# Seven quarter products for eight in ten of the eleven gate groups of the FFN behind the first attention

## The reference, cut to what matters

```
def swiglu(h, w_in, w_out):
    g, u = jnp.split(h @ w_in, 2, axis=-1)
    return (jax.nn.silu(g) * u) @ w_out

h = adaln(x, norm_g[i, 2], mod[:, 2, 0], mod[:, 2, 1])
x = x + 0.5 * (1.0 + mod[:, 2, 2][:, None, :]) * swiglu(h, ffn_w_in[i, 1], ffn_w_out[i, 1])
```

## Time and profile before

| what | value |
|---|---|
| median of 3 runs | 2938.61 us (2937.93 to 2938.81) |
| span of the profiled execution, first to last instruction | 2936.4 us |
| that execution's own time | not listed apart from its span; the median lies 2.2 us above the span |
| PE busy | 2916.7 us, 99% |
| PEld busy | 2426.8 us, 83% |
| DVE busy | 1646.2 us, 56% |
| ACT busy | 1148.2 us, 39% |
| POOL busy | 147.3 us, 5% |
| mean granted TensorE clock | 0.999 |

### The profile page before, as it was taken

One profiled execution on the slowest core, in us unless ns is written; L12 is line 12 of the kernel. 1 busy time (PEld: TensorE's weight loads), 2 busy tenths in 40 slices (PEclk: granted clock), 3 DMA queues, 4 the chain that ended last, 5 costly groups with the idle time before them and its releaser, 6 DMA issues. The chain is left out here.

```text
span 2936.4 us, 37187 instructions
## 1 busy us (share of the span) xinstructions
PE 2916.7 (99%) x14155; PEld 2426.8 (83%) x14155; DVE 1646.2 (56%) x2345; ACT 1148.2 (39%) x1592; POOL 147.3 (5%) x297
## 2 busy tenths in 40 slices
PE   9999999999999999999999999999999999999999
PEld 7888888888888888868888888778888888888887
DVE  8747486444653336876433357766535567854453
ACT  4223253222432225464332234564423338443332
POOL 0101001000010000040000000110000001000000
PEclk9999999999999999999999999999999999999999
DMA  7837326444362223252322222422322222323231
GB/s 299 276 130 254 132 91 219 170 165 151 123 217 97 96 98 106 86 175 70 115 93 101 93 79 94 151 90 87 107 97 95 98 90 79 108 94 102 91 103 69
DMA packets 100912, 366.53 MB, mean 125 GB/s; under 512 B 11248, under 2 KB 11808, under 8 KB 100784
## 3 DMA queue, kind: packets, MB, share of 16 engines
q1 hardware_dynamic: 77616, 276.56, 27.5%
q0 software_dynamic: 23168, 88.17, 8.8%
HBM read 362.51 MB, written 2.18 MB: 124 GB/s over the span
## 5 line engine op out<-in xcount | busy, mean ns | idle before, releaser
L1053 DVE TENSOR_TENSOR wl<-raw,wh 128x1024 fp32r<-128x1024 f32 x501 | 609.4, 1225 | 975.2 <-ACT wh L569 974.8
L569 ACT ACTIVATE wh<-raw 128x1024 fp32r<-128x1024 f32 x501 | 524.4, 1056 | 1196.4 <-PE PS L1797 1143.0
L1797 PE MATMUL PS<-HH,wh 128*128 128x512 f32 x2424 | 943.5, 389 | 0.5 <-DVE HL L1645 0.4
L1797 PE MATMUL PS<-HL,wh 128*128 128x512 f32 x2424 | 943.1, 389 | 0.0
L1797 PE MATMUL PS<-HH,wl 128*128 128x512 f32 x2424 | 943.0, 389 | 0.0
L1797 PEld LDWEIGHTS PS<-HH,wh 128*128 128x128 f32 x2424 | 455.1, 188 | 96.0 <-DVE HL L1645 0.8
L1797 PEld LDWEIGHTS PS<-HH,wl 128*128 128x128 f32 x2424 | 455.0, 188 | 94.5
L1797 PEld LDWEIGHTS PS<-HL,wh 128*128 128x128 f32 x2424 | 455.1, 188 | 94.0
L1797 PE MATMUL PS<-AH,wh 128*128 128x512 f32 x848 | 330.1, 389 | 0.5 <-DVEq L1680 0.5
L1797 PE MATMUL PS<-AL,wh 128*128 128x512 f32 x848 | 329.9, 389 | 0.0
L1797 PE MATMUL PS<-AH,wl 128*128 128x512 f32 x848 | 329.9, 389 | 0.0
(11 more groups left out here) (291 smaller groups left out, 3124.3 us busy)
## 6 DMA issues: line engine op xcount, KB each, us to landing
raw<-in_stream SPq DMA_DIRECT2D x501, 512.0 KB, 3.3
acc<-in_stream POOLq DMA_DIRECT2D x86, 512.0 KB, 4.8
piece<-in_stream POOLq DMA_DIRECT2D x42, 512.0 KB, 4.8
arena<-in_stream SPq DMA_DIRECT2D x16, 512.0 KB, 12.4
TBa<-negcum POOLq DMA_DIRECT2D x8, 640.0 KB, 5.2
TBa<-in_alibi POOLq DMA_DIRECT2D x8, 640.0 KB, 4.7
TBb<-negcum POOLq DMA_DIRECT2D x4, 640.0 KB, 4.3
piece<-negcum POOLq DMA_DIRECT2D x4, 640.0 KB, 6.0
```

Of the source, the lines that this page charges most:

```text
L569: F(wh[:, r, :], raw[:, r, :], ACT.Copy).then_inc(hi_done, 1)
L1053: TT(wl[:, r, :], raw[:, r, :], wh[:, r, :].bitcast(F32), ALU.subtract).then_inc(lo_done, 1)
L1797: mm = MM(PS[g % 2][:, j, :], l, x, start=(first and i == 0), stop=(last and i == 2), skip_group_check=after_halves)
```

## The change

Ten groups of the stage (the last five of the first half and all five of the second) are no longer done as 96 matmuls of 128 x 512. The product of one group is seen as a 2 x 2 product: the weights are split in four quarters (gate or value columns, first or second half of the depth; each quarter is one load of 128 x 1024), the activations in four quadrants (first or second half of the depth, first or second 256 tokens). Strassen's algorithm, in Winograd's form, gives the four quadrants of the result from seven products of sums of quarters. A product is 24 matmuls of 128 x 256: four tiles of depth, two blocks of columns, three passes. The first group of the first half stays as it was.

- Weight sums. Each quarter lies as it was loaded in one of six slots (two in `WK`, one each in `piece` and `bands`, two in `raw`). DVE adds and subtracts the quarters in place (four operations for a group, in `fast_low`), each right behind the low split of a product. Each of the seven operands is then split into high and low like a chunk and goes through the same ring of four slots.
- Input sums. Once for the stage, DVE rebuilds four quadrants from `HH` + `HL` (`whole`), forms four sums (`mixed_input`), ACT takes the high part of each (`mix_high`) and DVE the low part (`mix_low`). Three go to the new tiles `TH` and `TL`; the fourth replaces quadrant (first depth half, second token half) in `HH` and `HL`, when the plain group has used it.
- Results. Products are accumulated in three PSUM banks in the order 7, 6, 2, 5, product 1 of the next group, 3, 4. ACT copies product 1 from bank 0 to bank 1 ("seed"), copies the running value of bank 1 out twice, behind products 6 and 5, into `HT` or `PR`; DVE subtracts these from bank 2 behind products 5 and 4. In the diff `turn` is 1 for both halves, so `early`, the number of low splits ahead of `between`, is 2. ACT's Silu, DVE's multiply and the split of the hidden tiles follow as before.
- The stage's order. `split_until` is capped at the first chunk of the output map, so that no later chunk is split ahead of the products. At the end of a half the next products' place in the lists is taken by the chunks of the output map.

The core of the diff:

```
+FAST_SLOTS = 6
+FAST_BANK = {1: 0, 2: 0, 6: 1, 5: 1, 3: 1, 7: 2, 4: 2}
+FAST = {5: (5, 5)}
+def fast_order(n):
+    order = [(0, 1)]
+    for i in range(n):
+        order += [(i, 7), (i, 6), (i, 2), (i, 5)] + ([(i + 1, 1)] if i + 1 < n else []) + [(i, 3), (i, 4)]
+    return order, {p: k for k, p in enumerate(order)}
...
@@ SP @@
+            def load_fast(st, part):
+                first = NCH + NSUB * NADA + 4 * part["f"]
+                for m in range(4 * part["n"]):
+                    if m == 0:
+                        sp.wait_ge(h_ready, st["h"])
+                        sp.wait_ge(fast_lo, part["s"])
+                    elif m in (4, 5):
+                        sp.wait_ge(lo_done, part["c"] + m - 5)
+                    elif m >= FAST_SLOTS:
+                        sp.wait_ge(fast_lo, part["s"] + part["index"][fast_weight(m - FAST_SLOTS)] + 1)
+                    sp.dma_start(fast_raw(part, m), A["stream"][first + m, :, :]).then_inc(fast_in[m % FAST_SLOTS], 16)
...
@@ ACT @@
+            def fast_high(part, k):
...
+                if p in (1, 2, 4):
+                    act.wait_ge(fast_in[load % FAST_SLOTS], 16 * fast_loads(part, load))
+                else:
+                    act.wait_ge(fast_sum, 4 * (part["f"] + i) + {7: 1, 6: 2, 5: 3, 3: 4}[p])
+                if k >= RING:
+                    act.wait_ge(fast_used, part["s"] + k + 1 - RING)
+                else:
+                    act.wait_ge(chunk_used, part["c"] - RING + (k + part["turn"]) % RING + 1)
+                F(wh[:, (part["c"] + part["turn"] + k) % RING, :], fast_raw(part, load), ACT.Copy).then_inc(fast_hi, 1)
+            def fast_groups(st, part, between):
+                for k in range(RING):
+                    fast_high(part, k)
+                between()
+                for k, (i, p) in enumerate(part["order"]):
+                    act.wait_ge(fast_used, part["s"] + k + 1)
+                    if p == 1:
+                        F(ps[:, 1, :], ps[:, 0, :], ACT.Copy).then_inc(fast_seed, 1)
+                    elif p in (6, 5):
+                        F(prod[:, 0 if p == 6 else 1, :], ps[:, 1, :], ACT.Copy).then_inc(fast_copy, 1)
+                    elif p == 3:
+                        F(SG[:, :, :], ps[:, 0:2, :], ACT.Silu).then_inc(gate_act, 1)
+                    if k + RING < n:
+                        fast_high(part, k + RING)
+                    else:
+                        split_until(part["c"] + k + RING - n + 1)
+                    if p == 4:
+                        act.wait_ge(bank_free, part["g"] + i + 1)
+                        t = part["tile"] + 2 * i
+                        F(AH[:, t:t + 2, :].rearrange("p j (h t) -> p h j t", h=2),
+                          prod[:, :, :].rearrange("p h (j t) -> p h j t", j=2), ACT.Copy).then_inc(act_hi, 1)
...
@@ ACT, the stage: mix_high(0), (1), (2), then fast_groups with @@
+                                    mix_high(3)
+                                    hidden_group(st, e + u, g + u, c + 4 * u + 4, cv, j, 2 * u, 0)
...
@@ DVE @@
+            def fast_low(part, k):
+                dve.wait_ge(fast_hi, part["s"] + k + 1)
+                TT(wl[:, r, :], src, wh[:, r, :].bitcast(F32), ALU.subtract).then_inc(fast_lo, 1)
+                if p == 1:
+                    TT(a21, a21, a11, ALU.add).then_inc(fast_sum, 1)
+                elif p == 7:
+                    TT(a21, a21, a22, ALU.add).then_inc(fast_sum, 1)
+                    TT(a11, a21, a11, ALU.subtract).then_inc(fast_sum, 1)
+                elif p == 2:
+                    TT(a12, a12, a21, ALU.add).then_inc(fast_sum, 1)
+            def fast_groups(st, part, between):
+                early = RING - 1 - part["turn"]
+                for k in range(early):
+                    fast_low(part, k)
+                between()
+                for k in range(early, RING):
+                    fast_low(part, k)
+                for k, (i, p) in enumerate(part["order"]):
+                    if p in (5, 4):
+                        TT(prod[:, half, :], ps[:, 2, :], prod[:, half, :], ALU.subtract).then_inc(fast_up, 1)
+                    if p == 4:
+                        TT(prod[:, :, :], SG[:, :, :], prod[:, :, :], ALU.mult).then_inc(bank_free, 1)
+                    if k + RING < n:
+                        fast_low(part, k + RING)
+                    else:
+                        split_until(part["c"] + k + RING - n + 1)
+                    if p == 4:
+                        dve.wait_ge(act_hi, part["e"] + i + 1)
...
...
@@ DVE, the stage @@
+                                dve.wait_ge(h_ready, st["h"])
+                                whole(0, 0, 0)
+                                whole(0, 1, 1)
+                                mixed_input(0, mix_raw(0), mix_raw(1), ALU.subtract)
+                                whole(1, 1, 2)
+                                mixed_input(1, mix_raw(1), mix_raw(2), ALU.subtract)
+                                mix_low(0)
+                                mixed_input(2, mix_raw(4), mix_raw(2), None)
+                                mix_low(1)
+                                mix_low(2)
+                                whole(1, 0, 3)
+                                mixed_input(3, mix_raw(3), mix_raw(6), ALU.add)
+                                def between(u=plain_groups - 1, g=g, e=e, cv=cv, j=j):
+                                    hidden_group(st, e + u, g + u, cv, j, 2 * u, 0)
+                                    mix_low(3)
...
@@ PE @@
+            def fast_groups(st, part):
+                for k, (i, p) in enumerate(part["order"]):
+                    if p == 1:
+                        pe.wait_ge(bank_free, g - 1)
+                    elif p == 7 and k == 1:
+                        pe.wait_ge(mix_ready, 3)
+                    elif p == 6:
+                        pe.wait_ge(fast_seed, f + 1)
+                    elif p in (5, 3):
+                        pe.wait_ge(fast_copy, 2 * f + (1 if p == 5 else 2))
+                    elif p == 4:
+                        pe.wait_ge(fast_up, 2 * f + 1)
+                        pe.wait_ge(mix_ready, 4)
+                    pe.wait_ge(fast_lo, part["s"] + k + 1)
+                    for kk in range(4):
...
+                        for pair in range(2):
+                            MM(o, wh[:, r, w], xh, start=first, stop=False, skip_group_check=True)
+                            MM(o, wh[:, r, w], xl, start=False, stop=False, skip_group_check=True)
+                            mm = MM(o, wl[:, r, w], xh, start=False, stop=kk == 3, skip_group_check=True)
+                    mm.then_inc(fast_used, 1)
```

More of the change, by code:

```diff
@@ L313, in spread_bank, with fast_loads @@
             return {PAIRS - 2: 0, PAIRS - 1: 3}.get(i, 7)
+        def fast_loads(part, load):
+            slot = load % FAST_SLOTS
+            before_ = sum(len([m for m in range(4 * p["n"]) if m % FAST_SLOTS == slot]) for p in fast_parts if p["f"] < part["f"])
+            return before_ + load // FAST_SLOTS + 1
         def attend_bank(b, g):
             return PS[(g + b // 4) % 2][:, b % 4, :]
+        fast_parts = [part for st in plan for part in st.get("parts", ())]
+        fast_after = {part["c"] + m: part["s"] + part["total"] - 3 + m for part in fast_parts for m in range(RING)}
         negcum = nc.dram_tensor("negcum", (HEADS, SEG[4]), F32, kind="Internal").ap()
@@ L466, in _, with load_next @@
             sp.dma_start(bands[:, 0:NBAND], A["params"][:, NCOL:NCOL + NBAND]).then_inc(bands_in, 16)
[L467 to L474, removed]
+            def load_next(c):
                 sp.wait_ge(lo_done, c + 1 - RING)
@@ L476, in _, with load_chunks @@
                 load(c, c % RING)
+            def load_chunks(c, end):
+                whole, rounds = min(end, -(-c // RING) * RING), end // RING
+                for cc in range(c, whole):
+                    load_next(cc)
+                if rounds > whole // RING:
+                    with sp.Fori(whole // RING, rounds) as i:
+                        for r in range(RING):
+                            sp.wait_ge(lo_done, i * RING + (r + 1 - RING))
+                            load(i * RING + r, r)
+                for cc in range(max(whole, rounds * RING), end):
+                    load_next(cc)
@@ new lines, in _ @@
+            loaded = 2 * RING
+            for st in plan:
+                for part in st.get("parts", ()):
+                    load_chunks(loaded, part["c"])
+                    load_fast(st, part)
+                    for m in range(RING):
+                        if m >= 2:
+                            last = max(i for i in range(4 * part["n"]) if i % FAST_SLOTS == m + 2)
+                            sp.wait_ge(fast_lo, part["s"] + part["index"][fast_weight(last)] + 1)
+                        load_next(part["c"] + m)
+                    loaded = part["c"] + RING
@@ L559, in _ @@
         def _(act):
-            at = dict(split=0)
```

(18 more changed lines are left out.)

170 lines of the change are left out of this document (153 added, 17 removed).

## The result

| | before | changed |
|---|---|---|
| median | 2938.55 us (15 runs, 2937.93 to 2939.38) | 2944.74 us (15 runs, 2943.78 to 2946.13) |
| ratio | | 1.0021, 95% interval 1.0013 to 1.0028 |
| span of the profiled execution | 2936.4 us | 2944.1 us (its own time 2946.13) |

A forecast was written before the change was run, and what follows sets the result against it. PE, busy 2916.7 of 2936.4 us, was taken as the bound. Matmuls -16.0, start +18.7, clock +2.1 and ends +1.8 gave +6.6 us on 2938.6, so 2945.2 us; the 8-in-10 range was 2940 to 2950.

The forecast's parts named there:

- Matmuls, -16.0: Ten groups of products: 20.16 us a group in place of 21.76, 1.60 us back each, 16.0 us in all.
- The start, +18.7: Start of the stage: PE waits ahead of products 1 and 6 while DVE and ACT prepare operands, 18.7 us lost.
- The first part: Wait ahead of product 1 of the first group, behind DVE's input sums: product 1 starts 7.8 us late.
- The second: Chain from product 1's start through sums, high parts and the plain group's Silu to product 6, which starts at 1432.9.
- The clock, +2.1: First group, behind the wait ahead of product 6: 4.15 us at half speed lose 2.1 us; product 1's costs nothing.
- The ends, +1.8: Last group of each part: product 3 waits for ACT's copy of its bank, 0.9 us each, 1.8 for both.
- DVE and ACT in the steady groups, 0: Steady groups: DVE needs 17.4 us and ACT 11.3, both under PE's 20.16, so PE shouldn't wait.
- The rival in which DVE is the bound: Steady groups: DVE's lists exceed PE's time by 5%, ten groups lose 10 us, 2955; decides from about 2.7 more; 7%.
- the rule on the gap: Matmuls of products: the skill's estimate of 109 ns for 256 columns would save 2.4 us a group, 24 in all.
- the rival by the columns: Matmuls of products: columns alone set the distance, 0.113 us each, so the sum is -4.6 us, 2934.0; chance 3%.

The follow-up runs named there:

- products first: Changed kernel with DVE's low splits for products 6 and 2 and ACT's seed copy moved ahead of the plain group's hidden part: 2938.16 us, ratio 0.9998.
- Two plain groups: Changed kernel with two plain groups kept in the first half and nine groups as products, which also moved product 6's split forward: 2928.39 us, ratio 0.9964.
- kept busy: Changed kernel plus 34 unused bfloat16 matmuls between products 7 and 6 of the first group: 2942.36 us, ratio 1.0012.
- splits done twice: Changed kernel, low splits of two or four products repeated in the last four groups of each part: 2944.80 us with two, 2953.58 with four.

## Why the prediction was right

- *Matmuls, -16.0.* A steady group takes 20.16 us with PE full. The price of 256 columns, alone in the kernel before, came to +6.2 against 6.4 worked out. Nine groups in place of ten, without the long waits, make the stage 11.9 us shorter. By the starts of PE's matmuls that is -14.4 for the groups, +0.5 ahead of product 6, +0.2 ahead of product 2 and +1.9 at the two ends, -11.8 in all.
- *The start, +18.7.* 17.7 in the trace. The first part is right to 0.2 (7.6 for 7.8). The second was too long by 0.8. Counted from product 1's start, 0.5 of it had come by the end of the fourth high part, where operations in a row overlap by 0.1 each; 0.2 lies in the hidden part (1425.25 to 1431.23, 6.0 us for 6.2) and 0.1 in DVE's last two operations, which run at 1.14 each. Experiment "products first" shows that the second wait comes from the order of the lists. "Two plain groups" shows that both waits go when the start has 21.8 us more of cover and the third low split stands ahead of the hidden part; it doesn't show the place alone.
- *The clock, +2.1.* 5.27 - 2.88 = 2.4 in the trace and 2.4 by "kept busy". The clock came back 5.3 us after the work began, not 4.15 as in the earlier trace rows; behind product 1 it was about 4.2. Matmuls at the low clock follow at 0.213 us for 0.120, so a low stretch loses 0.44 of its length and not the half that was reckoned. The two errors work against each other, and with 1.4 to 2.4 us in four profiles the size of this term was hit in part by luck. That product 1's low clock costs nothing was right.
- *The ends, +1.8.* From 1525.22 to 1526.19 it takes 0.97 us where 0.12 is the distance, and to the next matmul 0.22: 0.95 at each end, 1.9 for both. The wait that the profile names (0.7) is the larger part of it.
- *DVE and ACT in the steady groups, 0.* 16.6 and 10.8 us for 17.4 and 11.3. Operations that follow each other overlap by about 0.1 us and are counted once there, which is about the size of the difference. The rival in which DVE is the bound needs between 2.5 and 5.0 us more for a group ("splits done twice"); the forecast's point was 2.7.
- The sum of the measured terms is -16.0 + 17.7 + 2.4 + 1.9 = +6.0, and the stage of the profile grew by 6.0, the median by 6.2. Misses of -1.0, +0.3 and +0.1 in the terms offset each other in part. That the median comes nearer to 6.6 than the stage does is no merit of the working: runs of this kernel spread over 2.4 us.
- One figure among the rivals is wrong: the rule on the gap doesn't give "half the amount" of the rival by the columns. With its 24 us the sum would be -24 + 22.6 = -1.4, against -4.6 for the columns alone and +6.6 forecast.

What stays open: the 1.6 us at the end of the two versions with two plain groups.

## What to carry to other kernels

An algorithm that saves an eighth of the multiplications pays 7% here, because a matmul of half the columns costs more than half (0.120 us for 0.2267); read that distance from the trace before counting operations. On an engine that is full, the work that prepares a new scheme must fit into the time in which the engine still does the old one: here 13.3 us of input sums had 7 us of cover and a chain of 16 us had 5.8. One plain group more, which also moved the third split ahead of the hidden part, turned +6 us into -10. Write the lists of all engines over the times of the trace before, name by name, at the place where the scheme begins; and count a wait of several us on PE with the low clock behind it, but only where the next thing due is PE's.

## What the runs showed of the hardware

- After PE's last matmul at 1409.94 the clock was still at 1.00 until about 1415 (0.88 in the window 1412 to 1416), at 0.50 when work began at 1417.77, and back at 1.00 at about 1421.9. 34 matmuls of bfloat16, unused, held it at 1.00 over the wait ahead of product 6. A wait of 2.5 us ahead of product 5 ("products first") left it at 1.00.
- Matmuls of 256 columns follow at 0.120 us at the upper clock and 0.213 at the lower (1418.34 to 1421.54, 15 of them): 1.78 times, not twice.
- The first matmul behind a short wait at the full clock is followed by the next after 0.22 us, not 0.12 (1526.19 to 1526.41).
- Two kernels that differ from others only in the middle of the program took 5.2 to 5.3 us from the last matmul to the end, the other eight 3.6 to 3.7.
